# First norm on token rows with the projection begun between turns, and the banded layer's norm in two VectorE operations a row

## The reference

```python
def first_block(x, norm_mix_g, w_in, ...):
    h = rms_norm(x, norm_mix_g[l])        # x * rsqrt(mean(x*x) + eps) * g
    z = h @ w_in[l]                       # 1024 x 2568
    ...
def second_block(x, c, ctx, c_ctx, w_mod, ...):
    for i in range(DEPTH_2):
        shift_x, scale_x, gate_x = split(silu(c) @ w_mod[i] + b_mod[i])
        shift_c, scale_c, gate_c = split(silu(c_ctx) @ w_mod[i] + b_mod[i])
        hx = modulate(rms_norm_2(x, norm_g[i]), shift_x, scale_x)
        hc = modulate(rms_norm_2(ctx, norm_g[i]), shift_c, scale_c)
        # layer 0: differential attention; layer 1: windowed attention:
        # qx, kx, vx, gx = split(hx @ w_in);  kc, vc = split(hc @ w_in)
```

## Time and profile before

| | us |
|---|---|
| median of 3 runs | 3183.47 (3180.57 to 3184.4) |
| the profiled execution, its own time | 3183.67 |
| its span in the profile | 3181.9 |
| TensorE matmuls busy in the span | 2936.7 (92%) |
| VectorE busy | 1730.8 (54%) |
| ScalarE busy | 982.2 (31%) |
| GpSimd busy | 1068.7 (34%) |

### The profile page before, as it was taken

The page is one execution under the profiler, slowest core; times in us unless marked ns, Lnnn a source line. Parts: engine busy times, 40 slices in busy tenths (PEclk is TensorE's granted clock), DMA queues, the critical chain, the costliest instruction groups (busy, mean ns, idle before and its releaser), DMA issues. The chain is left out here.

```text
span 3181.9 us, 44103 instructions
## 1 busy us (share of the span) xinstructions
PE 2936.7 (92%) x16440; PEld 2417.5 (76%) x16440; DVE 1730.8 (54%) x2485; ACT 982.2 (31%) x1727; POOL 1068.7 (34%) x657
## 2 busy tenths in 40 slices
PE   3989999999999999999999998888889599999998
PEld 2768787788888888778878878878778477867776
DVE  4744354574555545555566438788742553067753
ACT  1212263321111111131111117677730200167731
POOL 1623402555544455422222211323243432311221
PEclk9989999999999999999999999999999799999999
DMA  3434550111111111123344321212011132342111
GB/s 99 159 126 162 151 116 27 47 53 46 46 56 50 40 46 46 33 72 120 119 153 161 127 98 51 92 59 87 22 37 38 33 122 90 118 118 51 28 41 67
DMA packets 214040, 255.19 MB, mean 80 GB/s; under 512 B 9386, under 2 KB 182767, under 8 KB 213887
## 3 DMA queue, kind: packets, MB, share of 16 engines
q1 hardware_dynamic: 198306, 189.68, 20.0%
q10 hardware_dynamic: 15584, 63.51, 5.1%
HBM read 187.56 MB, written 65.60 MB: 80 GB/s over the span
## 5 line engine op out<-in xcount | busy, mean ns | idle before, releaser
L997 PE MATMUL ps<-hh,w_parts 128*128 128x512 f32 (+2 forms) x2560 | 999.1, 390 | 71.6 <-POOL hl L817 35.8
L998 PE MATMUL ps<-hl,w_parts 128*128 128x512 f32 (+2 forms) x2560 | 982.7, 384 | 0.0
L999 PE MATMUL ps<-hh,w_parts 128*128 128x512 f32 (+2 forms) x2560 | 981.0, 383 | 0.0
L997 PEld LDWEIGHTS ps<-hh,w_parts 128*128 128x128 f32 x2560 | 487.8, 191 | 188.8 <-issue 46.4
L778 POOL TENSOR_TENSOR w_parts<-w_raw,zero 128x1024 fp32r<-128x1024 f32 x140 | 292.0, 2085 | 948.9 <-PE ps L999 730.3
L998 PEld LDWEIGHTS ps<-hl,w_parts 128*128 128x128 f32 x2560 | 490.0, 191 | 104.2 <-issue 5.7
L999 PEld LDWEIGHTS ps<-hh,w_parts 128*128 128x128 f32 x2560 | 488.3, 191 | 99.2
L780 POOL TENSOR_TENSOR w_parts<-w_raw,w_parts 128x1024 fp32r<-128x1024 f32 x140 | 340.5, 2432 | 11.0
L1902 ACT ACTIVATE f_y<-f_z,convv 128x1024 f32<-128x1024 f32 x44 | 54.8, 1244 | 511.5 <-DVE f_z L2465 511.3
L2465 DVE TENSOR_TENSOR f_z<-ps,f_rs 128x1024 f32<-128x1024 f32 x44 | 53.9, 1224 | 181.4 <-PE ps L999 181.2
L2651 DVE TENSOR_SCALAR_CACHE_REDUCE b_s<-ps 128x640 f32<-128x640 f32 (+1 forms) x128 | 100.1, 782 | 95.6 <-PE ps L1543 95.6
(11 more groups left out here) (338 smaller groups left out, 4870.6 us busy)
## 6 DMA issues: line engine op xcount, KB each, us to landing
w_mod_sb<-in_w_mod SPq DMA_DIRECT2D x16, 1536.0 KB, 7.5
w_raw<-in_w_up SPq DMA_DIRECT2D x44, 512.0 KB, 3.7
w_raw<-in_a_w_in SPq DMA_DIRECT2D x32, 512.0 KB, 4.0
d_raw<-in_w_down SPq DMA_DIRECT2D x22, 512.0 KB, 4.4
w_raw<-in_w_in SPq DMA_DIRECT2D x20, 512.0 KB, 4.8
za_parts<-z_hi ACTq DMA_DIRECT2D x16, 640.0 KB, 3.0
za_parts<-z_lo ACTq DMA_DIRECT2D x16, 640.0 KB, 4.1
d_even<-za_parts SPq DMA_DIRECT2D x16, 640.0 KB, 7.0
```

The lines of the kernel that those rows point to most:

```text
L997: pe.matmul(out_, w_hi, x_hi, start=start, stop=False)
L998: pe.matmul(out_, w_hi, x_lo, start=False, stop=False)
L999: return pe.matmul(out_, w_lo, x_hi, start=False, stop=stop)
```

## The change

**First norm.** SP issues the identity, block 0 of x, the gain `tok_g` (1024 values repeated on all partitions), then the other blocks of x with the first two weight tiles among them, and only then the small constants and the context blocks; `tokrows` now has 10 buffers, one a block. For each block t ScalarE takes the sum of squares of each token along the row (`tok_ss`, Square with accumulation) and the root, VectorE the reciprocal and one operation `tok_h = tokrows * tok_rs * tok_g`. TensorE turns both the raw block (8 transposes, for `res`) and the normed one (8 more); ScalarE writes `hh` from PSUM, VectorE `hl` from PSUM; the copy to `res` alternates between ScalarE (even t) and VectorE (odd t). After the turns of blocks 4 to 7 TensorE does half a k-range of a first-pair tile on the first 512 latent columns (`first_tile`, 12 matmuls each). Then the small vectors are turned, and the other 512 columns of both tiles follow with the turns of the two context blocks between. The squares and sums of "mix", its spread, the per-row chain and POOL's share of it are gone. `w_mod_sb` is now loaded after the last context turn and the last constant (`consts_made` 10).

The core of the diff:

```diff
@@ the load queue
+            sp.dma_start(ident[:], const_ident).then_inc(tok_given, 16)
+            token_rows(0)
+            sp.dma_start(tok_g[:], norm_mix_g.broadcast_to([P, D])).then_inc(tok_given, 16)
+            for t in range(1, 4):
+                token_rows(t)
+            first_weights(0)
+            for t in range(4, 6):
+                token_rows(t)
+            first_weights(1)
+            for t in range(6, QB):
+                token_rows(t)
...
+            if begun:
+                raw_pair(1)
+                sp.wait_ge(tok_turned, 2 * QB + 3)
+                sp.wait_ge(consts_made, 10)
                 for s in range(2):
                     mod_tiles(0, s)
@@ TensorE
+            for t in range(QB):
+                turn_raw(t)
+                turn_normed(t)
+                if t in (4, 6):
+                    pe.wait_ge(w_split[t // 2 - 2], W0["gelu"][t // 2 - 2] + 1 + 1)
+                    pe.wait_ge(acc_free[t // 2 - 2], A0["gelu"][t // 2 - 2] + 1)
+                    pe.wait_ge(tok_dve, tok_parted(3))
+                if t >= 4:
+                    first_tile(t // 2 - 2, 0, range(t % 2 * 4, t % 2 * 4 + 4))
...
             for s in range(2):
+                first_tile(s, 1, range(KT)).then_inc(w_used[s], 1)
+                pe.wait_ge(tok_in[s], 16 * 3)
+                if s:
+                    pe.wait_ge(tok_dve, tok_parted(QB - 1) + 1)
+                turn_rows(6, tokrows[:, QB + s])
+            project(pe, "gelu", 8, LATENT_SEGS, 0, begun=True)
@@ ScalarE
+                    act.activation(junk[:, t % 4], tokrows[:, t].rearrange("p (k n) -> p k n", n=CTX), ACT.Square,
+                                   accum_out=tok_ss[:, t:t + 1]).then_inc(tok_act, 1)
+                    act.activation(tok_rs[:, t:t + 1], tok_ss[:, t:t + 1], ACT.Sqrt, bias=eps_1[:], scale=1.0 / D).then_inc(tok_act, 1)
+                if t:
+                    act.activation(hh[:, :, of], bank(b, 2).rearrange("p (k n) -> p k n", n=P), ACT.Copy).then_inc(tok_act, 1)
+                if t < QB and t % 2 == 0:
+                    act.activation(res[:, :, cols], bank(1, 2).rearrange("p (k n) -> p k n", n=P), ACT.Copy).then_inc(tok_act, 1)
@@ VectorE
+                    dve.reciprocal(tok_rs[:, t:t + 1], tok_rs[:, t:t + 1]).then_inc(tok_dve, 1)
+                    dve.scalar_tensor_tensor(tok_h[:, t % 2], tokrows[:, t], tok_rs[:, t:t + 1], tok_g[:], ALU.mult, ALU.mult).then_inc(tok_dve, 1)
+                if t:
+                    dve.tensor_tensor(hl[:, :, of], bank(b, 2).rearrange("p (k n) -> p k n", n=P), hh[:, :, of].bitcast(F32),
+                                      ALU.subtract).then_inc(tok_dve, 1)
+                if t < QB and t % 2:
+                    dve.tensor_copy(res[:, :, cols], bank(1, 2).rearrange("p (k n) -> p k n", n=P)).then_inc(tok_dve, 1)
...
-            norm_scale(dve, "b", ALL_COLS)
+            dve.tensor_tensor(c_g, res[:, :, 0:CTX], modg[:, 1, 1].unsqueeze(2).broadcast_to([P, KT, CTX]), ALU.mult).then_inc(ctx_step, 1)
+            for k in range(KT + 1):
+                if k < KT:
+                    dve.scalar_tensor_tensor(n_t[:, k % 2, 0:SEQ], res[:, k, X_COLS], modg[:, 1, 0, k:k + 1], n_rs[:, X_COLS],
+                                             ALU.mult, ALU.mult).then_inc(n_times[k % 2], 1)
+                if k:
+                    z = k - 1
+                    dve.scalar_tensor_tensor(hl[:, z, X_COLS], n_t[:, z % 2, 0:SEQ], mod[:, 24 + z, 0:1], hh[:, z, X_COLS].bitcast(F32),
+                                             ALU.add, ALU.subtract).then_inc(n_low[z % 2], 1)
+            dve.tensor_tensor(c_g, c_g, n_rs[:, 0:CTX].unsqueeze(1).broadcast_to([P, KT, CTX]), ALU.mult).then_inc(ctx_step, 1)
+            dve.tensor_tensor(c_g, c_g, mod[:, 24:24 + KT, 1:2].broadcast_to([P, KT, CTX]), ALU.add).then_inc(ctx_step, 1)
@@ POOL, between the first pair's splits and the second's
+                elif norm == "b":
+                    pool.wait_ge(ctx_step, 11)
+                    pool.tensor_tensor(hl[:, :, 0:CTX], c_g, hh[:, :, 0:CTX].bitcast(F32), ALU.subtract).then_inc(ctx_step, 1)
```

More of the change, by code:

```diff
@@ L255, in two_block_kernel @@
         lamt = alloc(scope, "lamt", [P, 4])
+        tok_h = alloc(scope, "tok_h", [P, 2, D])
+        tok_g = alloc(scope, "tok_g", [P, D])
+        tok_ss = alloc(scope, "tok_ss", [P, QB])
+        tok_rs = alloc(scope, "tok_rs", [P, QB])
         scope.close()
@@ L1224, in _ @@
-            for s in range(2):
-                turn_tokens(s, 0)
-            with pe.Fori(0, QB // 2) as i:
-                for s in range(2):
-                    turn_tokens(s, i + 1)
-            pe.wait_ge(rows_in, 16 * 14)
-            pe.transpose(bank(6)[:, 0:V_END], rows[0:V_END, :], ident[0:V_END, 0:V_END])
-            for n in range(2):
-                last = pe.transpose(bank(7)[:, n * 88:(n + 1) * 88], convrows[:, n, :], ident[0:88, 0:88])
-            last.then_inc(rows_turned, 1)
@@ new lines, in turn_normed, with first_tile @@
+            def turn_normed(t):
+                pe.wait_ge(tok_dve, tok_scaled(t))
+                turn_rows((6, 4)[t % 2], tok_h[:, t % 2])
+            def first_tile(s, seg, ks):
+                c0, w, p0 = LATENT_SEGS[seg]
+                for k in ks:
+                    wk = slice(k * P, (k + 1) * P)
+                    last = product(pe, acc[s][:, p0:p0 + w], wh[:, s, wk], wl[:, s, wk],
+                                   hh[:, k, c0:c0 + w], hl[:, k, c0:c0 + w], k == 0, k == KT - 1)
+                return last
```

167 lines of the change are left out of this document (98 added, 69 removed).

## The result

| | before | after |
|---|---|---|
| median of 4 runs each | 3183.93 us (3180.57 to 3188.11) | 3127.59 us (3125.00 to 3129.38) |
| ratio, 95% interval | | 0.9822 (0.9807 to 0.9838) |
| profiled execution; its span | 3183.67; 3181.9 us | 3129.38; 3127.3 us |

The kernel is 56.3 us faster by the medians and 54.6 us by the spans; 46.6 was forecast. The time lies in the range (3123 to 3151), 9 us under the point forecast. Three things are behind these 9 us: the start gave more than reckoned, so did the banded norm, and some of the gain was lost again in stages that the change doesn't touch.

The account below looks back on a forecast made before the run. TensorE, busy for 92% of the span, was taken as the bound, with two waits for a norm to shorten: 34.5 us at the start plus 12.1 in the banded norm, 46.6, giving 3136.9 us against the median, range 3123 to 3151.

Parts of the forecast that it names:

- the two events as clocks: First modulation sum (125.28 us before) and banded norm's tile (1,0) (2541.02 before): what comes earlier there leaves the stage earlier.
- First block, blocks 1 to 3: Start: tok_h of block 0 ready at 11.0 us, block 4's at 25.8, TensorE turning it from 29.5.
- the product of SBUF operands can take 2.62: Start, VectorE beside POOL's splits: product 2.62 us instead of 1.28; bounds 0 and 5.4, 2.0 taken behind block 7.
- Blocks 4 to 7: Start: TensorE longest, 16 transposes 3.8 us and 12 products 2.8, 6.6 a block, ending at 52.1.
- Modulation: End of start: load lands 7.2 us after issue, first tile takes 8.2, TensorE idles 5.5, sum at 87.1 us.
- Low clock: Start: slow products cost 1.5 us in tile (1,1) and 2.2 in blocks 4 to 7, cutting 38.2 to 34.5.
- Rival 1: Token stretch tighter: low clock throughout (7 us more), VectorE's 5.4 bound, or modulation 11.9; 3147 us, chance 0.15.
- rival 5: TensorE stays at the low clock through both stretches, start and banded norm; 16 us slower, 3199 us, chance 0.02.
- Banded norm: Rows 2.75 us apart, row 7 16.5 us earlier, tile (1,0) 12.1 us earlier behind POOL's context operation and split.
- rival 3: No low clock and no meeting of POOL and VectorE: gain 42 + 13.5, 3128 us, chance 0.09.
- Rival 2: Loads bound the start: at 5 us a block the stretch is 12 us longer, 3149 us, chance 0.05.
- rival 4: Banded norm's edit does nothing as POOL's split bounds it: gain there 8, 3141 us; within the forecast's 0.68.

Follow-up runs that it names:

- e1: The changed kernel with the banded norm of the kernel before, so only the new start; 3140.85 us, ratio 0.9864 to the kernel before.
- e2: The kernel before with only the new banded norm added; 3171.39 us, ratio 0.9960 to the kernel before.
- e6: The changed kernel with POOL's first weight splits held until VectorE has made tok_h of block 3; 3125.44 us.
- e4: The changed kernel with both context blocks turned ahead of the second halves of the first two tiles; 3118.89 us.
- e5: The changed kernel without products between the turns of blocks 4 to 7, both first halves put behind the last turn; 3141.02 us.
- e3: The changed kernel with POOL's context operation in the banded norm moved behind the splits of the second weight pair; 3121.54 us.
- e9: The changed kernel with POOL's second d_hi of the ffn stage's first chunk held until VectorE's f_y is done; 3121.80 us.

## Why the prediction was right, and where its numbers failed

**What bounds, and the two events as clocks:** right. The halves add (e1, e2), and each gave what its event said (45.4 and 15.4) less some 3 us that were lost later: 42.8 and 12.3.

**First block, blocks 1 to 3:** 11.0 and 29.5 for the first product against 10.97 and 29.39. The second agreement is luck. The step "the product of SBUF operands can take 2.62" cost 2.7 us here, which I had booked behind the blocks. Two things gave as much back: turns at 1.04 to 1.30 from block 1 on saved some 0.6, and behind block 4's `tok_h` stood one turn (27.83 to 29.39, 1.56 us) where the forecast put 16 transposes of 3.65, since the raw block had been turned before. Without the meetings two blocks take 6.9 and 7.4 (e6, `tok_h` turned at 10.94, 17.80 and 25.22).

**Blocks 4 to 7:** the step that failed. "TensorE is longest: 16 transposes 3.8 with the hand-off" took the duration from the earlier trace rows, where TensorE stood idle before each group. Measured 1.67 for both turns (33.49 to 35.16). A block is 4.5 instead of 6.6, and the blocks end at 47.1 instead of 52.1 (54.1 with the term for POOL, which belonged further ahead). The same mis-sized term gives 1.8 of the 2.8 us between there and the last context turn (13.3 instead of 16.1). Together, 5.0 at the end of the blocks, the 2.0 booked there for POOL and 2.8 behind them make 9.8 of the 10.2 us by which the first sum is earlier than forecast (76.91 against 87.1).

**Modulation:** right in each part: load 6.9 (7.2), tile 8.2 (8.2), idle 5.3 (5.5). The Trainium skill (SBUF — State Buffer, "Who interferes with whom") says that issue order decides who blocks. The changed kernel agrees: VectorE came first, it kept 8.2 and POOL took 11.56. But the order in which the trace starts them doesn't settle every meeting. In e4 POOL's split at 60.78 started within VectorE's run, as the one at 75.12 does here, and kept 2.10, while VectorE's 14 operations took 11.28 instead of 7.49. Which of the two a start within a run will be was not found out, so the 8.2 was the likelier value and not a sure one.

**Low clock:** 3.7 was taken off. Measured 1.2 in the first products (6 of them 0.43 apart), and 3.0 between the sums: the sum takes 2.72 instead of 1.50, and 9 products 0.2 more each. Rival 1, the low clock throughout, was wrong, and so was rival 5: the interleaved stretch from 33 to 50 us has 17.00 of 17 us busy, and its turns and products go at the upper level. The page that spoke for rival 5 (the Trainium skill, TensorE: Matmul & The Clock Gate, "HAM oscillation — how this bites in real kernels") describes stretches with waits between the groups. Here there are none from the first product at 29.39 to the wait for the modulation. In e5, with waits of 0.2 to 2.5 us between its turns, the turns from 32 us on went at the upper level and 8 products behind them at the lower. Windows of the changed kernel follow. The first columns are the stretch, its length and TensorE's busy time and count; the last three are the granted clock, the DMA share and the GB/s:

```profile
7.00:16.00 9.00, 6.74 (x32) 6.10 (x32) 4.82 (x6) 7.12 (x13) 3.23 (x2) 1.00 1.07 395
...
26.00:33.00 7.00, 6.90 (x26) 6.21 (x27) 4.92 (x6) 4.59 (x8) 0.00 (x0) 0.57 0.48 144
33.00:50.00 17.00, 17.00 (x102) 14.61 (x101) 10.14 (x21) 8.42 (x12) 0.00 (x0) 1.00 0.00 0
```

My "against" for rival 1, the 1.00 in the earlier trace rows, was no evidence: the turns of that window are all of the slow kind. In the first line here the column again says 1.00 while the turns take 1.97.

**Banded norm:** 15.0 against 12.1 earlier. The mis-sized term is the row, forecast at 2.75 and measured at 2.52 (VectorE's two operations of 1.28 stand back to back; ScalarE, 1.15 and not 1.23, and the hand-offs are hidden behind them): row 7 at 20.2 instead of 23.2. From row 7 to tile (1,0) it was 16.4 against 16.2, each operation in its forecast place. e3 shows what that step left out: the idle time ahead of (1,0) costs a second time through the clock.

**The rest:** wrong by omission. I took the lead at the first sum to reach the end. 3.7 us of it went in the ffn stage (e9). Another 2.6 went behind the banded norm; other traces show there anything from a loss of 2.8 (e2) to a gain of 0.9 (e5), so this part is no more than a lead can tell, and it was not followed up. The two places gave 45.4 + 15.4 = 60.8 us by the leads; less 6.3 that is 54.5, against 46.6. The range held by luck in part. The start gave 45.4, or 42.8 as a whole kernel (e1), beyond the 40 that bounded it, and only the unforeseen losses brought the sum back inside: 60.8 us of gain would have been 3122.7. The bounds themselves (40 and 16.5) end at 3127; the 3123 of the range has no term behind it.

**The split into rivals:** the result lies at rival 3's time (3128), and for other reasons. Neither of its conditions held, since both the low clock and the meeting of POOL and VectorE were there. Rival 2 (loads) and rival 4 (nothing from the banded norm) are out: TensorE waited for no load from 7.0 to 140 us, and the banded norm gave 15.0.

## What to carry to other kernels

Before a duration of TensorE is carried from one stretch to another, look at what the engine did just before it in each: here a turn measured between waits cost up to 1.9 times what it cost in a full stretch, and an idle stretch of 5.0 to 5.3 us cost its length and then 9 to 12 products at half pace, one of 0.25 us nothing more. When work is pulled forward, ask of each operation that others wait for (a context turn, a split of weights) what stands ahead of it in its queue without feeding it: two reorderings of that kind gave 6.0 and 8.7 us here and took no added work. A shift of some 40 us changed who came first at a meeting of VectorE and POOL, in a stage that nobody edited, so compare the lead stage by stage and not at the end alone.
